# A gMLP and sliding-window decoder trunk on one core: V of the first mixer as seven block products

## The reference

```
u, v, z = split(h @ w_in, 3)             # w_in: 1024 x 6144, each part 2048 wide
u = gelu(u);  v = layer_norm(gelu(v))    # over the 2048 of a row
mixed = einsum("gts,bnsgc->bntgc", tril(w_s), v in chunks of 128) + b_s
y = u * mixed * silu(z)
x = x + gate * (y @ w_out)               # w_out: 2048 x 1024
```

## Time and profile before

| | us |
|---|---|
| median of three runs | 2292.11 |
| profiled execution | 2294.21 |
| its span, first to last instruction | 2292.5 |
| TensorE matmuls busy | 2229.3 (97%) |
| VectorE busy | 1107.5 (48%) |
| ScalarE busy | 947.7 (41%) |
| GpSimd busy | 910.1 (40%) |

### The profile page before, as it was taken

The page is one execution under the profiler, slowest core; times in us unless marked ns, Lnnn a source line. Parts: engine busy times, 40 slices in busy tenths (PEclk is TensorE's granted clock), DMA queues, the critical chain, the costliest instruction groups (busy, mean ns, idle before and its releaser), DMA issues.

```text
span 2292.5 us, 28322 instructions
## 1 busy us (share of the span) xinstructions
PE 2229.3 (97%) x10726; PEld 1872.7 (82%) x10726; DVE 1107.5 (48%) x1563; ACT 947.7 (41%) x1822; POOL 910.1 (40%) x576
## 2 busy tenths in 40 slices
PE   5999999999999999999999999998999999999998
PEld 4788888888888888888888888786888888887886
DVE  6744532314724411654231453436667656656754
ACT  4334352535453434444253445323444434444442
POOL 2445454454553445454445455420222232232222
PEclk9999999999999999999999999999999999999999
DMA  9653442543554443465344365658686787776654
GB/s 344 262 175 124 154 177 92 175 149 113 186 201 177 135 173 116 158 213 198 110 138 160 102 211 202 257 219 318 220 313 215 284 335 240 263 294 247 220 202 165
DMA packets 205159, 460.68 MB, mean 201 GB/s; under 512 B 17152, under 2 KB 93024, under 8 KB 204640
## 3 DMA queue, kind: packets, MB, share of 16 engines
q1 hardware_dynamic: 202064, 453.58, 55.7%
q10 hardware_dynamic: 2960, 5.30, 0.6%
HBM read 359.19 MB, written 90.18 MB: 196 GB/s over the span
## 4 chain that ended last, share of the span: by engine, by line
PE 90%; DMA 4%; DVE 3%; issue 1%; SPq 1%; ACT 0%; POOLq 0%; DVEq 0%; ACTq 0%; POOL 0%
PE ps L1562 27%; PE ps L1564 27%; PE ps L1563 27%; PE ps L1727 2%; PE ps L1765 1%; PE ps L1766 1%; DVE acc L1190 1%; PE ps L1791 1%; DMA r<-kv_input 1%; DMA r<-b_input 1%; DMA w_raw<-in_a_w_out 1%; DMA r<-oz_kept 1%; PE ps L1800 1%; PE ps L1801 1%; PE ps L1803 1%
## 5 line engine op out<-in xcount | busy, mean ns | idle before, releaser
L744 POOL TENSOR_TENSOR w_lo<-w_raw,w_hi 128x1024 fp32r<-128x1024 f32 x256 | 646.1, 2536 | 761.1 <-ACT w_hi L868 761.0
L868 ACT ACTIVATE w_hi<-w_raw 128x1024 fp32r<-128x1024 f32 x256 | 271.0, 1060 | 620.7 <-DMA w_raw<-in_a_w_in 395.0
L1562 PE MATMUL ps<-h,w_hi 128*128 128x512 f32 x1024 | 401.7, 392 | 0.0
L1564 PE MATMUL ps<-h,w_lo 128*128 128x512 f32 x1024 | 398.8, 389 | 0.0
L1563 PE MATMUL ps<-h,w_hi 128*128 128x512 f32 x1024 | 398.6, 389 | 0.0
L817 POOL TENSOR_SCALAR_AFFINE_SELECT pt<-pt 128x512 fp32r<-128x512 f32 x128 | 82.4, 643 | 397.7 <-ACT pt L1121 344.9
L1564 PEld LDWEIGHTS ps<-h,w_lo 128*128 128x128 f32 x1024 | 192.2, 188 | 40.5
L1563 PEld LDWEIGHTS ps<-h,w_hi 128*128 128x128 f32 x1024 | 192.4, 188 | 39.2 <-issue 0.2
L1562 PEld LDWEIGHTS ps<-h,w_hi 128*128 128x128 f32 x1024 | 192.3, 188 | 39.3 <-issue 0.2
L1562 PE MATMUL ps<-w_hi,h 128*128 128x512 f32 x512 | 201.1, 393 | 4.6 <-DVE h L1218 4.6
L1562 PE MATMUL ps<-w_hi,y_hl 128*128 128x512 f32 x512 | 201.7, 394 | 2.1 <-POOL w_lo L744 2.1
(11 more groups left out here) (214 smaller groups left out, 3997.8 us busy)
## 6 DMA issues: line engine op xcount, KB each, us to landing
w_raw<-in_a_w_in SPq DMA_DIRECT2D x256, 256.0 KB, 3.1
w_hi<-b_weights_split SPq DMA_DIRECT2D x104, 512.0 KB, 4.3
w_lo<-b_weights_split SPq DMA_DIRECT2D x104, 512.0 KB, 5.6
w_raw<-in_a_w_in SPq DMA_DIRECT2D x64, 512.0 KB, 4.7
w_raw<-in_a_w_out SPq DMA_DIRECT2D x64, 512.0 KB, 4.1
kv_input<-xks SPq DMA_DIRECT2D x32, 512.0 KB, 6.8
b_input<-hbs SPq DMA_DIRECT2D x32, 512.0 KB, 7.6
r<-b_input SPq DMA_DIRECT2D x16, 1024.0 KB, 11.0
```

What stands on the lines that cost most here:

```text
L744: g.tensor_tensor(wlo[p][:, rows_], raw[p][:, rows_], whi[p][:, rows_].bitcast(F32), ALU.subtract).then_inc(w_lo, 1)
L868: s_.activation(whi[p][:, rows_], raw[p][:, rows_], ACT.Copy).then_inc(w_hi, 1)
L1562: t_.matmul(dst_, stat[0], mov[0], start=start, stop=False)
L1564: return t_.matmul(dst_, stat[1], mov[0], start=False, stop=stop)
```

## The change

In groups two to four the product of h with two slabs of w_v (512 positions, 1024 inputs, 1024 columns: `sv` = 0 and 1) is cut 2 x 2 x 2 into blocks and computed with seven block products in place of eight (Winograd's form of Strassen's scheme). Each takes 256 positions (two chunks), 512 inputs and 512 columns: 4 pieces, in banks 0 and 1 or 2 and 3 in turn.

- Left factors: four blocks or combinations of h. Four sums s1 to s4 of the blocks of h are formed on GpSimd, rounded on ScalarE, and their remainders formed on GpSimd. h is kept whole for this (`hfw`).
- Right factors: three of the seven are blocks of w_v, loaded raw and split as before ("B"); four are combinations ("T"), formed once in group one (VectorE four subtractions, ScalarE rounding, GpSimd two remainders for each of 8 row tiles), stored as hi and lo in DRAM, and loaded as such, 2.1 MB a unit.
- Outputs: ScalarE copies product 0 to `ut`, VectorE adds each further product from PSUM to running sums in SBUF; gelu now reads these sums in place.
- Moved: the rope tables of groups two to four from the uz stages into VectorE's second half of V; x1's scaling from slab 0 to the second half of V; the next x (load, squares, scale) from the V and uz phases to the start and end of the output phase; the store of x1 behind the loads of V's fourth unit; mixer B's splits from stages 1, 2 and 6 to 10 to stages 4 to 10 in groups two to four.

The core of the diff (PE, DVE, ACT, POOL and SP programs):

```
+V_UNITS = [8] + [14] * (NG - 1)
+FACTORS = [("B", 0, 0), ("T", 2), ("T", 3), ("B", 1, 0), ("T", 0), ("B", 1, 1), ("T", 1)]
+COMB_STAGES = [4, 5, 6, 7, 8, 9, 10, 10]
 # SP
+                if kept_split(u):
+                    sv, m = product_of(u)
+                    for part, w in ((0, whi[p]), (1, wlo[p])):
+                        sp.dma_start(w[:, 2 * hh:2 * hh + 2].bitcast(F32), cbd[sv, FACTORS[m][1], hh, part]) \
+                            .then_inc(raw_in[2 * p + hh], 16)
...
+                    for n in range(2, V_UNITS[i]):
+                        unit(v_unit(i, n))
+                        if n == 3:
+                            for cnk in range(NC):
+                                sp.wait_ge(ao_read, at("ao_read", i - 1, cnk + 5))
+                                sp.dma_start(x1d[i - 1, :, cnk], x1[:, cnk, :]).then_inc(x1_out, 16)
 # POOL
+                    pool.wait_ge(piece_done, pieces(ao_unit(i - 1, 3, 1), 8))
+                    pool.wait_ge(xt_full, at("xt_full", i, 8))
+                    s_sums(0)
+                    pool.wait_ge(h_hi, at("h_hi", i, 8))
+                    s_sums(1)
+                    s_rest(i, 0)
+                    for q in range(2):
+                        s_add(3, q, h_block(0, 0, q), ALU.subtract, h_block(1, 0, q))
+                    lo(v_unit(i, 3))
+                    s_rest(i, 1)
+                    s_rest(i, 2)
+                    lo(v_unit(i, 5))
+                    s_rest(i, 3)
                     x1_stage(i - 1)
+                    lo(v_unit(i, 7))
+                    lo(v_unit(i, 10))
+                    lo(v_unit(i, 12))
 # ACT
+                def v_blocks(sv):
+                    for c in range(2):
+                        act.wait_ge(piece_done, pieces(v_unit(i, 7 * sv), 3 + c))
...
+                        s_.activation(ut[:, c, :], bank(2 * sv + c), ACT.Copy).then_inc(first_kept, 1)
+                    if sv == 0:
+                        s_round(i, 1)
+                        s_round(i, 2)
+                    hi(v_unit(i, 7 * sv + 3))
+                    if sv == 0:
+                        s_round(i, 3)
+                        x1_squares(i - 1)
+                    for c in range(2):
+                        gelu(sv, c, 2 * sv, 7 + c)
+                    hi(v_unit(i, 7 * sv + 5))
+                    for c in range(2):
+                        gelu(sv, c, 2 * sv + 1, 11 + c)
+                    for u in (v_unit(i, 7),) if sv == 0 else (uz_unit(i, 0, 0),):
+                        hi(u)
 # DVE
+                    block_out(sv, 1, (flat(ue), flat(ut)))
+                    if sv == 0:
+                        dve.wait_ge(s_sum, 8 * i)
+                    else:
+                        table(i, 0)
+                    block_out(sv, 2, (flat(uu), flat(ut)), (flat(ue), flat(ue)))
+                    if sv == 1:
+                        x1_scale(i - 1)
+                    block_out(sv, 3, (lambda c: v_chunk(j, c), flat(ut)))
+                    if sv == 1:
+                        table(i, 1)
+                    block_out(sv, 4, (flat(uu), flat(uu)))
+                    for c in range(2):
+                        v_stat(j, c, 8 * sv + c + 1)
+                    block_out(sv, 5, (lambda c: v_chunk(j + 1, c), flat(uu)))
 # PE
+                    for m in range(PRODUCTS):
+                        u, b = v_unit(i, 7 * sv + m), (0 if m % 2 == sv else 2)
+                        def bank_free(c):
...
+                            elif m == 2:
+                                pe.wait_ge(first_kept, 4 * (i - 1) + 2 * sv + c + 1)
+                            else:
+                                pe.wait_ge(block_sum, sums(i, sv, {3: 1 + c, 4: 4 + 2 * c, 5: 7 + c, 6: 9 + c}[m]))
```

More of the change, by code:

```diff
@@ L36, with group_of, v_unit, uz_unit @@
 PI_BELOW = 3.1415925
-U_V, U_UZ, U_AO, A_UNITS = 0, 8, 24, 32
-FIRST_B = A_UNITS * NG
+V_UNITS = [8] + [14] * (NG - 1)
+FIRST = [sum(V_UNITS[:i]) + 24 * i for i in range(NG + 1)]
+FIRST_B = FIRST[NG]
+PRODUCTS = 7
+FACTORS = [("B", 0, 0), ("T", 2), ("T", 3), ("B", 1, 0), ("T", 0), ("B", 1, 1), ("T", 1)]
+def group_of(u):
+    return max(i for i in range(NG) if FIRST[i] <= u)
+def v_unit(i, n):
+    return FIRST[i] + n
+def uz_unit(i, g, ku):
+    return FIRST[i] + V_UNITS[i] + 2 * g + ku
+def ao_unit(i, k, n):
+    return FIRST[i] + V_UNITS[i] + 16 + 2 * k + n
+def product_of(u):
+    if u >= FIRST_B:
+        return None
+    i = group_of(u)
+    n = u - FIRST[i]
+    return (n // PRODUCTS, n % PRODUCTS) if i >= 1 and n < V_UNITS[i] else None
+def kept_split(u):
+    product = product_of(u)
+    return product is not None and FACTORS[product[1]][0] == "T"
 def b_order():
@@ L66, with pieces_in @@
 B_PIECES = 8 * len(B_UNITS)
+SPLIT_HERE = {u: n for n, u in enumerate(w for w in range(FIRST_B) if not kept_split(w))}
+def pieces_in(u):
+    return 4 if product_of(u) is not None else 8
+PIECES_BY = [0]
+for _u in range(UNITS):
+    PIECES_BY.append(PIECES_BY[-1] + pieces_in(_u))
 PRO_SLOTS, STEPS, TAIL_SLOTS = 6, 16, 7
@@ L807, in _ @@
                 else:
[L808 to L809 removed]
+                    lo(v_unit(i + 1, 0))
             x1_stage(NG - 1)
@@ L945, in _ @@
             for i in range(NG):
[L946 to L954, removed]
-                        s_.activation(dst_[:, :, cnk, :], bank(cnk).rearrange("p (g n) -> p g n", g=2),
-                                      ACT.Gelu_apprx_tanh).then_inc(v_gelu, 1)
-                    hi(first + 2 * j + 3)
-                    split(i, j)
@@ L959, in _ @@
-                if i == 0:
+                if i == 0:
+                    for j in range(4):
+                        hi(v_unit(0, 2 * j + 2))
+                        for cnk in range(NC):
+                            act.wait_ge(piece_done, pieces(v_unit(0, 2 * j + 1), 2 * cnk + 2))
+                            s_.activation(v_chunk(j, cnk), bank(cnk).rearrange("p (g n) -> p g n", g=2),
+                                          ACT.Gelu_apprx_tanh).then_inc(v_gelu, 1)
+                        hi(v_unit(0, 2 * j + 3))
+                        comb(0, j)
@@ L1628, in spatial_row_sums, with unit @@
                 last.then_inc(pe_pro, 1)
-            def unit(u, piece, bank_free=None, after=None):
-                for k in range(8):
+            def unit(u, piece, bank_free=None, after=None, half_there=None):
+                for k in range(pieces_in(u)):
                     j, hh = order(u, k)
-                    if k in ((0, 4) if by_halves(u) else (0, 1)):
-                        pe.wait_ge(w_lo, 2 * u + hh + 1)
+                    if k in starts(u):
+                        if kept_split(u):
+                            pe.wait_ge(raw_in[2 * (u % 2) + hh], landed(u))
+                        else:
+                            pe.wait_ge(w_lo, 2 * SPLIT_HERE[u] + hh + 1)
+                        if half_there is not None:
+                            half_there(hh)
                     if hh == 0 and bank_free is not None:
```

421 lines of the change are left out of this document (303 added, 118 removed).

## The result

The changed kernel takes 2321.13 us (median of four runs, 2318.32 to 2325.05); the kernel before took 2291.49 beside it (2290.44 to 2296.37). The ratio is 1.0126, with a 95% interval of 1.0104 to 1.0148: slower, 5 us above the widest range that I had given (2270 to 2316) and 18 above the forecast's own (2286 to 2303). The profiled execution has a span of 2317.3 us against 2292.5, so 24.8 us are to be found.

A forecast was written before the change was run, and what follows sets the result against it. TensorE, busy 97% of the span, was taken to bound the kernel. 2294.2 - 32.6 (matmuls) + 34.2 (A to E) + 1 (the rest) = 2296.8, 2295 us as a median; own range 2286 to 2303, widest 2270 to 2316.

The forecast's parts named there:

- Matmuls removed: V in groups two to four: 64 pieces become 56, 10.9 us less a group, 32.6 us in all.
- A: Product 3 in V: its raw weights, behind two kept units in the stream, come 1.2 us late a group.
- B: Product 5 in V: raw weights behind x1's store and product 4's weights come 2.0 us late a group.
- C: Product 11 in V: VectorE's first rope table delays the bank-freeing block sums; 1.7 us a group (0 to 4).
- D: Product 12 in V: x1's scaling, sums and gelus delay the rounding of its weights; 4.7 us a group (3 to 7).
- E: First uz unit after V: second table, sums and gelus delay its weights; 1.8 us a group (0 to 3).
- Rival 3: GpSimd's sums take 2.4 us each or it serves VectorE's locks in turn: 2310 and up; chance 0.08.
- TensorE waits nowhere by this; I put down 1 us, 0 to 8: Group one's combinations and output phase: GpSimd still delivers weights in time; 1 us put down, 0 to 8.
- Rival 1: V's stalls mostly don't come, tables find GpSimd quiet: 2275 at 5 us a group, 2270 at 3.2; chance 0.30.
- Rival 2: The weight stream sets V's pace, sustained rate below about 380 GB/s, 17 us a group: 2311; chance 0.20.
- Rival 4: Combinations back up GpSimd in group one, 8 us once: 2303; chance 0.05.
- The rule on 358 GB/s: V's weight loads limited by HBM to some 358 GB/s: near 5 us more a group, so 2310.

The follow-up runs named there:

- experiment 1: Changed kernel with the rope tables of groups two to four back in the uz stages: 2294.45 us, ratio 1.0007 to the kernel before.
- Experiment 4: Kernel before, with 14 or 19 extra ScalarE copies ahead of the weight rounding at three uz stages of every group: 2327.03 us (1.0143) and 2376.74 us (1.0360).
- 19 copies: Kernel before, with 19 ScalarE copies of 128x512 ahead of the weight rounding at three uz stages per group: 2376.74 us, ratio 1.0360.
- versions 4 and 5: Changed kernel, tables in uz, sums before combinations, one combination a stage, later x load; x1's store split behind units 3, 5, 6, 7 (2286.01 us) or behind 3 (2286.86).
- half the kept bytes: Changed kernel without loading the lo part of the kept combinations, 8.4 MB less per V phase: 2305.75 us, ratio 1.0047 to the kernel before.
- 14 copies: Kernel before, with 14 ScalarE copies of 128x512 ahead of the weight rounding at three uz stages per group: 2327.03 us, ratio 1.0143.

## Why the prediction was wrong, step by step

*Matmuls removed: right.* 32.7 us against 32.6; the pace within V is the old one wherever TensorE does not wait.

*The waits in V: their sum right (33.2 of 34.2 us), place by place for the most part.* In us, groups two, three, four:

| step | product | predicted | measured |
|---|---|---|---|
| A | 3 | 1.2 | 1.53, 1.63, 1.54 |
| B | 5 | 2.0 | 1.87, 2.01, 1.83 |
| C | 11 | 1.7 | 1.44, 1.18, 0.94 |
| D | 12 | 4.7 | 4.46, 4.45, 3.99 |
| E | first uz unit | 1.8 | 0, 0.2, 0 |
| none | 1 | none | 1.69, 1.45, 1.25 |
| none | 4 | none | 1.03, 0.27, 0.67 |

D's chain is the one that I laid out, link for link, in the rows above, and experiment 1 showed what starts it. E is not there. The V phases, which I had put at 86 to 88 us, took 91.3, 91.5 and 90.1 (87.2 before): the waits that I had forecast, and the slow matmuls that I had not. Products 1 and 4, with kept weights, are waits that I had not placed. TensorE's rows at the starts of products 1, 3, 4 and 5 in group two of the kernel after:

```profile
441.02 0.47 PE L1897 MATMUL ps<-w_hi,h 128*128 128x512 f32 x1 [1.53 <-issue]
...
453.54 0.50 PE L1897 MATMUL ps<-w_hi,h 128*128 128x512 f32 x1 [1.37 <-POOL w_lo L906]
...
460.14 0.50 PE L1897 MATMUL ps<-w_hi,s 128*128 128x512 f32 x1 [0.87 <-DMA w_lo<-v_weights_combined]
...
467.58 0.50 PE L1897 MATMUL ps<-w_hi,s 128*128 128x512 f32 x1 [1.71 <-POOL w_lo L906]
```

SP issues product 1's first loads at 433.99, when the last output unit has let go of their buffer; product 0 takes 5.44 us, but the second of the two 0.5 MB transfers lands at 440.93, and product 1 starts at 441.02. I had laid out the landing of raw halves and taken kept weights to be in time because nobody has to split them. That the total agrees is thus partly luck: E and the two missing places cancel.

The sizes of A and B are luck as well. The raw halves that they wait for landed 16.2 and 30.2 us after the start of V in group two, not 14.0 and 26.8; but the late products 1 and 4 had moved the times at which they were wanted by nearly as much. The stream was slow mostly at its start (windows of the kernel after, columns as in the earlier trace rows):

```profile
434.00:440.00 6.00, 5.49 (x25) 4.18 (x23) 4.91 (x5) 2.13 (x4) 5.68 (x4) 1.00 0.65 225
440.00:450.00 10.00, 8.98 (x40) 7.46 (x41) 1.38 (x2) 3.72 (x8) 8.94 (x8) 1.00 1.03 401
...
434.00:464.00 30.00, 26.23 (x114) 20.75 (x113) 10.23 (x13) 14.74 (x25) 24.40 (x17) 1.00 0.94 358
```

I had taken 410 GB/s from 2 us after the first issue on.

*GpSimd's sums: right.* Bounds were 1.2 and 2.4 us, I took 1.2. GpSimd's row in the kernel after, in the first V phase with seven products:

```profile
438.83 1.28 POOL L935 TENSOR_TENSOR s4f<-hfw,s2f 128x512 f32<-128x512 f32 x1 [0.16 <-issue]
```

The others lie between 1.26 and 1.74, the longer ones beside VectorE's work. Rival 3 is out; no wait at product 2.

*"TensorE waits nowhere by this; I put down 1 us, 0 to 8": this is the step that failed.* Group one cost 12.1 us and the output phases 2.8. I had asked whether GpSimd delivers weights in time with its 17 to 22 us of work in a stage of 23.6, and it nearly does. I had not laid out VectorE's queue there, although and the paragraph on C say that each of its operations on SBUF waits for GpSimd's: 21 of the 32 subtractions took 1.7 to 2.9 us instead of 0.7, in front of the sums on `wz`, and y_hl's remainders beside the double combination. The rule was in the working and was used for V alone.

*A term that was missing: the lower clock behind a wait.* 8.3 us in V and 4.3 in group one, 12.6 together. The sum priced a wait at its own length. Experiment 4 shows that this holds for the short ones and fails for the long: with 19 copies 56.5 us of waits brought 22 more. The earlier trace rows could have warned only by its one wait; the trace of before has long waits at its start, and I did not look at the matmuls behind them (after the one of 4.65 us that ends at 37.73, six or so are slow, 1.3 us in all).

These two terms, 11.1 + 2.8 over the 1 us put down and 12.6 counted once (4.3 of it lies in group one's 12.1), make 13.9 + 8.3, the 22.2 us (24.8 - 2.6) by which the spans miss the forecast; the 3.3 of short gaps and the 1.0 and 2.2 the other way cancel.

*The range.* The bounds that I had given for A to E add up to 3 to 21 us a group, not 5 to 19, and the upper end of 2316 left out the 8 us that I had allowed for the rest. With 19 and 8 it would have been 2324, with the measured 2321 inside; the account of group one would have been as wrong.

*The rivals.* Rival 1 (stalls of 3.2 to 5 us a group, 2270 to 2275) did not come in the change, and versions 4 and 5 go some of the way: with the tables out of V 5 to 6.5 us a group are left. Its "for" was wrong, though: 48% busy on VectorE said nothing about the 20 us in which tables, scaling and sums stood in one queue. Rival 2, with 2311 the nearest in time, was the wrong reason: V moved 284 GB/s at a DMA share of 0.78 in group two, and half the kept bytes left D whole. It is part of the truth: the first 30 us of V ran below its 380 GB/s (358), the waits up to product 5 came to 5.3 to 6.1 us a group where A and B were to make 3.2, and half the bytes took 18 us off, most of it at products 1 to 5. Rival 4 named the place, the combinations in group one, at 8 us and with a chance of 0.05; it should have been priced through VectorE.

*The rule on 358 GB/s* in the Trainium skill ("DMA: Bandwidth & Descriptors", Where 436 GB/s comes from) would by the prediction have made A 2.3 us and product 4 late by 1.2. Here A is 1.5 to 1.6 and product 4 late by 0.3 to 1.0, but that is no test of the rule, as the slow start of the stream moved both. From 440 to 450 us V moved 401 GB/s at a full share, so the trace disagrees with the rule here too.

*The rule that I left unused.* The rows of VectorE at 2.4 to 2.9 us beside GpSimd's are what the Trainium skill describes in "SBUF — State Buffer" (Who interferes with whom), where one of the two engines holds the port while the other waits. The rows agree. Group one adds what happens with two full queues: they alternate, one operation each.

## What to carry to other kernels

When work is given to GpSimd, lay out VectorE's queue at the same place: each of its operations with both sides in SBUF can last as long as GpSimd's beside it (here 2.4 to 2.9 us instead of 0.43 to 0.69), and the room that busy shares promise is not there. Before a block of small vector work is moved next to a phase whose units were just halved, ask what it stands in front of; here tables that cost nothing in the uz stages cost 27 us in V. Price a long wait of TensorE above its length, by the matmuls behind such a wait in the same kernel's trace.

## What the runs showed of the hardware that I had not expected

- Waits of TensorE of 0.8 to 1.9 us (24 with 14 copies, and those in V) had no slow matmuls behind them; waits of 3.7 to 5.7 us had 6 to 11 matmuls at 0.43 instead of 0.227 us, granted clock 0.54, 1.3 to 2.4 us more. From 1.93 to 3.57 us both happened.
- VectorE and GpSimd with full queues on SBUF alternate: 10.81 us for four operations of 0.69, beside GpSimd's at 2.8 instead of 2.40.
- A wait removed can bring another, and a wait added can take one away: with the store of x1 moved, 11.1 us of waits appeared at product 9, those at products 4, 5, 11 and 12 went, and the whole was 13 us shorter by the ratios (7 by the profiled spans).
